# Gated linear attention in a decoder step: the output of a head computed with tokens on the partitions instead of features

## The chip, the cores and the metric

The kernel runs on one core of a Trainium2 chip. It is written by hand in a low-level language: each engine (PE for matrix multiplication, DVE for vectors, ACT for activation functions, POOL for general work, SP for issuing DMAs) has its own list of instructions, which it runs strictly in order, and the lists meet only at semaphores. The metric is the device time of one launch in microseconds (us), from the first to the last instruction with what lies around it. The profile is one execution of the same program, taken by the hardware profiler.

## The reference

The program is one inference step of a two-layer decoder: a layer with gated linear attention (GLA), then a layer with stick-breaking attention over keys and values that eight sampled sequences read from a paged cache. What matters here is the end of the GLA layer, for a prompt of 512 tokens, 4 heads, keys of 128 and values of 256 features per head, in chunks of 64 tokens:

```python
o_intra = jnp.einsum('bhnij,bhnjv->bhniv', att, vc)
chunk_kv = jnp.einsum('bhnck,bhncv->bhnkv', kc * jnp.exp(b_last - b), vc)
def step(s, inp):
    dcy, kv = inp
    return dcy[..., None] * s + kv, s
s_final, s_starts = lax.scan(step, s0, (decay, chunk_kv))     # moveaxis left out
o_inter = jnp.einsum('bhnck,bhnkv->bhncv', q_in, s_starts)
o = o_intra + o_inter
...
o = rms_norm(o, g_out).reshape(B, L, GLA_DV) * jax.nn.silu(g)  # the norm is over the 256 features of a head
return o @ w_out, s
```

So for each head: a causal product inside each chunk, eight states (128 x 256) that follow from one another, their product with the queries, a norm of each token's 256 output features, the gate, and then the product with `w_out`.

## The kernel before

Activations lie feature-major: features on the 128 partitions, the 512 tokens along a row. The program runs in stages of eight products each ("q", "k", "v", "g", "wo0", "ple0", "q1", ...), a product being one tile of 128 output features for all tokens. PSUM has eight banks of 512 float32 columns; the products take banks 0 to 3 in turn, so that up to four of them can wait for DVE to read them, and banks 4 to 7 serve the rest. All matrix products are float32: either split into three fp32r products (line L1562, stages q to g), or done natively in two passes, which the trace shows as two MATMUL records each (L1546 in wo0, ple0, q1; all of the GLA's own products).

The GLA's output is computed inside stage "g". It has eight steps u = 0 to 7 on PE, one product each; head h = u // 2. In an even step PE runs the product, then the output of the head before (`gla_output(h - 1)`) and the scores of head h (`gla_scores`: the decayed keys turned to token-major in bank 4, and `gla_inside` in bank 5). In an odd step it runs the product and then the states of head h (`gla_states`: eight small products of keys with values, four at a time in banks 6 and 7, because the outputs need the same banks), with the square sum of head h - 1 between the two halves (`gla_square_sum`: a product with a matrix of ones, which leaves the sum over the features on every partition of bank 4). The last head's output and square sum lie inside stage "wo0", between pieces of its first products: those need the gated output of a head, feature tile by feature tile (`wait_x`, the semaphore `x_hi`; tiles 0 to 3 are heads 0 and 1, tiles 4 and 5 head 2, tiles 6 and 7 head 3).

DVE in a step: `split_lo` of a weight tile (L1067), `normed` (L1090, the product out of PSUM times the norm), in an odd step `state_steps` (L1272 and L1275: a copy and seven multiply-adds, each waiting for the one before), then `silu` (L1308), then in an odd step `gate_o` of the head before (L1283 to L1287: two products of the output with the norm's factor, two with the gate). In an even step copy_predicated (L1311) masks the scores. Between them DVE scores pages of the key cache for the sampled sequences (`score_pages`, L1244: a reduction of 128 x 1024, and for some pages the multiplication L1243). POOL multiplies most pages with the query (L599) as soon as a page has landed; a page's slot is loaded again once it has been reduced, and four slots serve stage "g". Before the pages of stage wo0 POOL waits for the last head's gate (`gated`), and SP waits for `o_mm` of the last head before it loads pages into the four slots that lie over the GLA's buffers. ACT in an odd step: sigmoid (L689), then `o_rms` of the head before (L823 and L824: Ln, Exp, each with a table load); in an even step sigmoid, `o_copies` of the head before (L816 to L819: two squares, two copies out of banks 6 and 7) and a copy of the turned keys (L850). After step 7: `x_hi` (L662) of tiles 4 and 5, `o_copies` and `o_rms` of the last head, `x_hi` of tiles 6 and 7.

Behind wo0, PE starts ple0 and must add the last square sum (`add_squares(1, KT - 1)`, L1598) before the norm, which DVE and ACT need to go on; in wo0 each product is followed by one such sum.

## Time and profile before

| | us |
|---|---|
| median of 3 runs | 919.36 (919.06 to 919.89) |
| span of the profiled execution, first to last instruction | 917.2 |
| what the median has beyond this span | 2.2 |
| PE busy | 871.6 (95%) |
| DVE busy | 569.6 (62%) |
| ACT busy | 450.9 (49%) |
| POOL busy | 278.1 (30%) |

Times in the rows below are counted from the first instruction of the profiled execution. A row of the timeline merges neighbouring instructions of one line: start, duration, engine, line, operation, what is written from what is read, shape, count, and in square brackets how long the engine stood idle before it and what it waited for. Two neighbouring operations of one engine overlap by some 0.1 us in these rows, so what an operation costs in a sequence is read from start to start. Stage "g" with the GLA's output ends at about 253 us, the first products of wo0 end at 287.7, and ple0's first product ends at about 347.

### The profile page before, as it was taken

How to read it: one execution, taken by the hardware profiler on the slowest of the kernel's cores; microseconds unless marked ns; L12 is line 12 of the kernel's file. 1: busy time of each engine (PE TensorE's matmuls, PEld its weight loads, DVE VectorE, ACT ScalarE, POOL GpSimd, SP SyncE). 2: the span in 40 equal slices, each digit the busy share in tenths (PEclk: the TensorE clock that was granted, in tenths of full speed). 3: DMA queues.
4: the chain of work that ended last, by engine and by line, in shares of the span. 5: the costliest groups of instructions: out<-in, count | busy, mean ns of one | idle time of the engine just before them, and what ended most of it. 6: DMA issues, size and time to landing. Idle time of an engine off the chain costs nothing.

```text
span 917.2 us, 14970 instructions
## 1 busy us (share of the span) xinstructions
PE 871.6 (95%) x5141; PEld 608.2 (66%) x5141; DVE 569.6 (62%) x680; ACT 450.9 (49%) x1521; POOL 278.1 (30%) x148
## 2 busy tenths in 40 slices
PE   5999999989999998999996999999989999999995
PEld 3666777877754444444475887877845554799995
DVE  4555285878957858988998542222167777553553
ACT  4501482324467667568874231221277776434433
POOL 3000002944429997985775000000100000021110
PEclk9989999999999999999998999999999999999997
DMA  9798977752479988888999149989888879321202
GB/s 327 269 374 315 370 235 274 240 179 81 143 235 386 393 292 281 299 294 307 380 330 321 40 147 343 326 315 341 305 317 291 318 267 360 119 92 47 92 1 94
DMA packets 109308, 232.49 MB, mean 253 GB/s; under 512 B 7410, under 2 KB 66425, under 8 KB 109233
## 3 DMA queue, kind: packets, MB, share of 16 engines
q1 hardware_dynamic: 50736, 171.64, 51.6%
q10 hardware_dynamic: 58496, 59.90, 19.6%
q8 instruction: 41, 0.67, 0.3%
q14 instruction: 35, 0.28, 0.1%
HBM read 220.38 MB, written 11.14 MB: 252 GB/s over the span
## 4 chain that ended last, share of the span: by engine, by line
PE 72%; ACT 8%; DVE 7%; DMA 7%; POOL 2%; issue 2%; SPq 1%; ACTq 0%; DVEq 0%; POOLq 0%
PE pp L1559 19%; PE pp L1562 11%; PE pp L1546 10%; PE pp L1970 6%; PE pp L1927 4%; ACT slot L793 3%; PE pp L1543 3%; DMA s<-in_state_gla_dram 3%; DMA slot<-in_cache_k_dram 3%; PE pp L1954 2%; PE pp L1523 2%; POOL slot L599 2%; PE pp L1941 2%; PE pp L1574 1%; PE pp L1639 1%
## 5 line engine op out<-in xcount | busy, mean ns | idle before, releaser
L599 POOL TENSOR_TENSOR slot<-slot,qb 128x1024 f32<-128x1024 f32 x94 | 247.5, 2659 | 128.1 <-DMA slot<-in_cache_k_dram 76.8
L793 ACT ACTIVATE slot<-slot 128x64 f32<-128x64 f32 x480 | 114.8, 241 | 29.5 <-POOL slot L599 29.5
L1244 DVE TENSOR_REDUCE zall<-slot 128x16 f32<-128x1024 f32 x98 | 118.0, 1214 | 11.0 <-POOL slot L599 9.8
L1067 DVE TENSOR_TENSOR w_lo<-w_raw,w_hi 128x1024 fp32r<-128x1024 f32 x57 | 77.5, 1361 | 71.3 <-ACT w_hi L651 71.2
L651 ACT CAST w_hi<-w_raw 128x1024 fp32r<-128x1024 f32 x58 | 60.5, 1044 | 68.1 <-PE pp L1562 26.0
L793 ACT ACTIVATION_READ_ACCUMULATOR slot<-slot 128x1 f32 x480 | 90.0, 188 | 0.0
L1546 PE MATMUL pp<-xn,w_raw 128*128 128x512 f32 x192 | 86.3, 603 | 0.2 <-ACT xn L662 0.2
L1546 PE MATMUL pp<-xn,w_unsplit 128*128 128x512 f32 x192 | 83.9, 592 | 0.0
L1562 PE MATMUL pp<-xa_hi,w_hi 128*128 128x512 f32 x200 | 82.5, 412 | 0.0
L1562 PE MATMUL pp<-xa_hi,w_lo 128*128 128x512 f32 x200 | 80.0, 400 | 0.0
L1562 PE MATMUL pp<-xa_lo,w_hi 128*128 128x512 f32 x200 | 79.7, 399 | 0.0
L1559 PE MATMUL pp<-xb_hi,w_hi 128*128 128x260 f32 x384 | 78.8, 286 | 0.0
L1559 PE MATMUL pp<-xb_lo,w_hi 128*128 128x260 f32 x384 | 77.0, 282 | 0.0
L1559 PE MATMUL pp<-xb_hi,w_lo 128*128 128x260 f32 x368 | 74.0, 283 | 0.0
L1243 DVE TENSOR_TENSOR slot<-slot,qb 128x1024 f32<-128x1024 f32 x34 | 69.9, 2055 | 0.0
L1546 PEld LDWEIGHTS pp<-xn,w_raw 128*128 128x128 f32 x192 | 36.8, 193 | 44.7 <-issue 43.7
L1546 PEld LDWEIGHTS pp<-xn,w_unsplit 128*128 128x128 f32 x192 | 36.5, 190 | 44.2 <-issue 44.0
L1424 DVE TENSOR_TENSOR_SCAN pcum<-pcum,ones 128x256 f32<-128x256 f32 (+1 forms) x64 | 49.3, 813 | 24.8 <-ACT psig L949 24.8
L1970 PE MATMUL pp<-slot,zs 128*32 128x512 f32 x480 | 61.5, 598 | 0.6 <-DVE g1T L1368 0.6
L1559 PEld LDWEIGHTS pp<-xb_hi,w_hi 128*128 128x128 f32 x384 | 59.0, 188 | 1.2 <-issue 0.8
L1559 PEld LDWEIGHTS pp<-xb_lo,w_hi 128*128 128x128 f32 x384 | 59.1, 188 | 0.0
L1090 DVE TENSOR_TENSOR work<-pp,rstd 128x512 f32<-128x512 f32 (+1 forms) x32 | 22.2, 694 | 59.3 <-PE pp L1559 34.4
(302 smaller groups left out, 1516.6 us busy)
## 6 DMA issues: line engine op xcount, KB each, us to landing
slot<-in_cache_k_dram SPq DMA_DIRECT2D x128, 512.0 KB, 6.1
slot<-in_cache_v_dram SPq DMA_DIRECT2D x120, 512.0 KB, 5.3
w_raw<-in_gla_w_in_dram ACTq DMA_DIRECT2D x12, 1024.0 KB, 7.5
slot<-in_gla_w_in_dram SPq DMA_DIRECT2D x24, 512.0 KB, 10.3
w_raw<-in_w_kv_dram ACTq DMA_DIRECT2D x8, 1024.0 KB, 10.5
w_raw<-in_w_ple_gate_dram ACTq DMA_DIRECT2D x6, 1024.0 KB, 5.1
s<-in_state_gla_dram SPq DMA_DIRECT2D x1, 4096.0 KB, 27.2
out_dram<-s ACTq DMA_DIRECT2D x4, 1024.0 KB, 9.3
```

The lines of the kernel that those rows point to most:

```text
L599: nc.gpsimd.tensor_tensor(slot[s][:], slot[s][:], qb[:, (n // NPG) % 2, :], ALU.mult).then_inc(S("k_mul_pool"), 1)
L651: nc.scalar.copy(hi, raw).then_inc(S("w_hi"), 1)
L793: ins = nc.scalar.activation(part, part, ACT.Copy, accum_out=zall[:, n % NPG, b * SH + h:b * SH + h + 1])
L1067: nc.vector.tensor_tensor(lo, raw, hi.bitcast(F32), ALU.subtract).then_inc(S("w_split"), 1)
L1243: own.then(nc.vector.tensor_tensor(at, at, qb[:, b % 2, :], ALU.mult))
L1244: nc.vector.tensor_reduce(zall[:, n % NPG, b * SH:(b + 1) * SH], at.rearrange("p (h d) -> p h d", d=HD), AX.X, ALU.add).then_inc(S("k_used ...
L1424: own.did(nc.vector.tensor_tensor_scan(rev, rev, ones[:, 0:1].to_broadcast([P, n]), 1.0, ALU.mult, ALU.mult))
L1546: last = nc.tensor.matmul(bank[banks_of(j)[0]], w[:, k, :], x[:, 0:NP_TOK], start=(k == 0), stop=(k == KT - 1))
L1559: last = nc.tensor.matmul(pp[m % 2][:, t, 0:H2], w[:, k, :], x[:, t * H2:(t + 1) * H2], start=(k == 0 and first), stop=(k == KT - 1 and w ...
L1562: last = nc.tensor.matmul(bank[banks_of(j)[0]], w[:, k, :], x[:, 0:NP_TOK], start=(k == 0 and first), stop=(k == KT - 1 and w is wl))
L1927: last = nc.tensor.matmul(bank[bk][:, c0:c0 + n], qz[i % 4][:, h % 2, q * P:(q + 1) * P], K1T[:, i, 0:n], start=False, stop=True, skip_gro ...
L1970: last = nc.tensor.matmul(pp[3][32 * g:32 * g + 32, t, :], zs[:, c:c + 32], slot[SLOT_OF[e0 + g]][:, t * 512:(t + 1) * 512], start=(j0 == ...
```

## The change

The output of a head is now made token-major: rows are tokens, columns its 256 features, one block of 128 tokens per half bank (`o_block`). `gla_output` takes the masked scores as the stationary operand and the values as the moving one (4 products of 128 x 256), and then, for each chunk after the first, the queries (64 columns) as stationary and the state (256 columns) as moving operand, written to the 64 partitions of the chunk. ACT's squares, one for each block, also give the sum along the row (`accum_out`), so the product with ones goes; `o_rms` is one Sqrt of 4 numbers per partition. DVE takes the reciprocal and scales the four blocks in place in SBUF (`scale_o`, TENSOR_SCALAR), PE turns them back with eight transposes (`gla_turned`) into banks 4 and 5 (the last head 6 and 7), and `gate_o` is two products that read them from there. Since the square sum and its bank are gone from the odd step, the chunks 4 to 7 of a head get banks 4 and 5, and PE issues the eight state products in one piece.

```diff
         def chunk_bank(c):
-            return bank[6 + c % 2][:, (c // 2 % 2) * HV:(c // 2 % 2 + 1) * HV]
+            return bank[(6 if c < 4 else 4) + c % 2][:, (c // 2 % 2) * HV:(c // 2 % 2 + 1) * HV]
+        def o_block(b):
+            return bank[6 + b // 2][:, (b % 2) * HV:(b % 2 + 1) * HV]
+        def o_rows(h, b):
+            return (qT, kT)[b // 2][:, h, (b % 2) * HV:(b % 2 + 1) * HV]
...
# ACT
                 act.wait_ge(S("o_mm"), h + 1)
-                if h:
-                    act.wait_ge(S("oss_mm"), h)
-                nc.scalar.activation(work[:, 0, 0:NP_TOK], bank[6], ACT.Square)
-                nc.scalar.activation(work[:, 1, 0:NP_TOK], bank[7], ACT.Square).then_inc(S("o_sq"), 1)
+                for b in range(TB):
+                    own.did(nc.scalar.activation(work[:, b // 2, (b % 2) * HV:(b % 2 + 1) * HV], o_block(b), ACT.Square,
+                                                 accum_out=ossq[:, TB * h + b:TB * h + b + 1]))
                 nc.scalar.copy(qT[:, h, :], bank[6])
                 nc.scalar.copy(kT[:, h, :], bank[7]).then_inc(S("o_out"), 1)
             def o_rms(h):
-                act.wait_ge(S("oss_mm"), h + 1)
-                own.then(nc.scalar.activation(gkT[:, h, :], bank[4], ACT.Ln, bias=epsc[:], scale=1.0 / HV))
-                nc.scalar.activation(gkT[:, h, :], gkT[:, h, :], ACT.Exp, scale=-0.5).then_inc(S("o_root"), 1)
+                own.wait()
+                nc.scalar.activation(ort[:, TB * h:TB * h + TB], ossq[:, TB * h:TB * h + TB], ACT.Sqrt, bias=epsc[:],
+                                     scale=1.0 / HV).then_inc(S("o_root"), 1)
...
                     nc.scalar.copy(kdtok[:, h % 2].rearrange("p b n -> p (b n)"), bank[4]).then_inc(S("kd_out"), 1)
-                elif h:
-                    o_rms(h - 1)
+                    if h:
+                        o_rms(h - 1)
+            act.wait_ge(S("st_step"), GH * NCH)
+            o_copies(GH - 1)
+            o_rms(GH - 1)
             act.wait_ge(S("gated"), GH - 1)
             for i in range(4, KT - 2):
                 x_hi(KT + i, gT[:, i, :])
-            act.wait_ge(S("st_step"), GH * NCH)
-            o_copies(GH - 1)
-            o_rms(GH - 1)
             act.wait_ge(S("gated"), GH)
# DVE
+            def scale_o(h):
+                dve.wait_ge(S("o_root"), h + 1)
+                dve.wait_ge(S("o_out"), h + 1)
+                own.then(nc.vector.reciprocal(orstd[:, TB * h:TB * h + TB], ort[:, TB * h:TB * h + TB]))
+                for b in range(TB):
+                    last = nc.vector.tensor_scalar(o_rows(h, b), o_rows(h, b), orstd[:, TB * h + b:TB * h + b + 1], None, ALU.mult)
+                last.then_inc(S("o_n"), 1)
             def gate_o(h):
-                dve.wait_ge(S("o_root"), h + 1)
-                r = gkT[:, h, :]
-                nc.vector.tensor_tensor(qT[:, h, :], qT[:, h, :], r, ALU.mult)
-                own.then(nc.vector.tensor_tensor(kT[:, h, :], kT[:, h, :], r, ALU.mult))
-                for vt, o in enumerate((qT, kT)):
+                dve.wait_ge(S("o_t"), h + 1)
+                for vt in range(2):
                     g = gT[:, 2 * h + vt, :]
-                    last = nc.vector.tensor_tensor(g, g, o[:, h, :], ALU.mult)
+                    last = nc.vector.tensor_tensor(g, bank[(4 if h < GH - 1 else 6) + vt], g, ALU.mult)
                 last.then_inc(S("gated"), 1)
...
                     normed(j, gT[:, u, :])
+                    if h >= 2:
+                        gate_o(h - 2)
                     score_pages(j)
...
                 elif h:
-                    gate_o(h - 1)
+                    scale_o(h - 1)
+            gate_o(GH - 2)
+            scale_o(GH - 1)
             gate_o(GH - 1)
# PE
                 if h >= 2:
-                    pe.wait_ge(S("o_root"), h - 1)
+                    pe.wait_ge(S("gated"), h - 1)
+                if h:
+                    pe.wait_ge(S("st_step"), h * NCH)
...
+            def gla_states(h):
+                pe.wait_ge(S("kd_out"), h + 1)
+                pe.wait_ge(S("att_out"), h + 1)
+                if h:
+                    pe.wait_ge(S("o_out"), h)
+                for c in range(NCH):
...
             def gla_output(h):
                 pe.wait_ge(S("st_step"), (h + 1) * NCH)
+                for b in range(TB):
+                    nc.tensor.matmul(o_block(b), attT[:, h % 2, b * P:(b + 1) * P], vtok[:, b, h * HV:(h + 1) * HV],
+                                     start=(b % 2 == 0), stop=False, skip_group_check=True)
+                for c in range(1, NCH):
+                    r = (c % 2) * CH
+                    last = nc.tensor.matmul(o_block(c // 2)[r:r + CH, :], qT[:, h, c * CH:(c + 1) * CH], states[:, c - 1, :],
+                                            start=False, stop=(c == NCH - 1), skip_group_check=True)
+                last.then_inc(S("o_mm"), 1)
+            def gla_turned(h):
+                pe.wait_ge(S("o_n"), h + 1)
+                if h < GH - 1:
+                    pe.wait_ge(S("st_step"), (h + 2) * NCH)
                 for vt in range(2):
                     for b in range(TB):
+                        last = nc.tensor.transpose(bank[(4 if h < GH - 1 else 6) + vt][:, b * P:(b + 1) * P],
+                                                   o_rows(h, b)[:, vt * P:(vt + 1) * P], ident[:])
+                last.then_inc(S("o_t"), 1)
-            def gla_square_sum(h):
-                pe.wait_ge(S("o_sq"), h + 1)
-                pe.wait_ge(S("kd_out"), min(h + 2, GH))
-                for vt in range(2):
-                    last = nc.tensor.matmul(bank[4], ones[:], work[:, vt, 0:NP_TOK], start=(vt == 0), stop=(vt == 1))
-                last.then_inc(S("oss_mm"), 1)
...
                 if u % 2 == 0:
+                    if h >= 2:
+                        gla_turned(h - 2)
                     if h:
                         gla_output(h - 1)
                     gla_scores(h)
...
-            product(PHASES["wo0"][0], KT, wait_x=True, tiles=range(4))
+            wo = PHASES["wo0"][0]
+            product(wo, KT, wait_x=True, tiles=range(4))
+            gla_turned(GH - 2)
             gla_output(GH - 1)
-            product(PHASES["wo0"][0], KT, wait_x=True, tiles=range(4, 6))
-            gla_square_sum(GH - 1)
-            product(PHASES["wo0"][0] + 1, KT, tiles=range(6))
+            product(wo + 1, KT, tiles=range(4))
             pe.wait_ge(S("p_in"), 16)
+            pe.wait_ge(S("gated"), GH - 1)
             embedded(pin0, 1, 5).then_inc(S("pt"), 1)
-            pe.wait_ge(S("o_root"), GH)
             embedded(pin0, 0, 4).then_inc(S("pt"), 1)
-            product(PHASES["wo0"][0], KT, wait_x=True, tiles=range(6, KT))
-            product(PHASES["wo0"][0] + 1, KT, tiles=range(6, KT))
+            product(wo, KT, wait_x=True, tiles=range(4, 6))
+            product(wo + 1, KT, tiles=range(4, 6))
+            product(wo + 2, KT, tiles=range(6))
+            gla_turned(GH - 1)
+            product(wo, KT, wait_x=True, tiles=range(6, KT))
+            product(wo + 1, KT, tiles=range(6, KT))
+            product(wo + 2, KT, tiles=range(6, KT))
             for u in range(8):
+                if u >= 3:
+                    product(wo + u, KT)
                 if u >= 2:
-                    product(PHASES["wo0"][0] + u, KT)
-                if u:
-                    add_squares(1, u - 1)
+                    add_squares(1, u - 2)
+            add_squares(1, KT - 2)
```

How the lists stand now. On PE, the odd step 5 and the even step 6 of stage "g" (the products L1562, after the change L1580, are left out): before,

```order
L1795 MATMUL pp<-vtok,kdtok 128x256 [waits o_out,kd_out]
L1818 MATMUL pp<-work,ones 128x512 [waits kd_out,o_sq]
L1795 MATMUL pp<-vtok,kdtok 128x256 [waits st_step]
...
L1804 MATMUL pp<-attT,vtok 128x128 [waits st_step,att_out]
L1808 MATMUL pp<-qT,states 128x64 x7
L1804 MATMUL pp<-attT,vtok 128x128 x4
L1808 MATMUL pp<-qT,states 128x64 x7
L1773 MATMUL pp<-ident,kT 128x128 [waits o_root,kdec]
```

and after, where L1813 are the states, L1835 the turning (of the head two back), L1820 and L1824 the output (of the head before), L1793 the turned keys:

```order
L1813 MATMUL pp<-vtok,kdtok 128x256 [waits o_out,att_out,kd_out]
L1813 MATMUL pp<-vtok,kdtok 128x256 x7
...
L1835 MATMUL pp<-ident,qT 128x128 [waits st_step,o_n]
L1835 MATMUL pp<-ident,qT 128x128
L1835 MATMUL pp<-ident,kT 128x128 x2
L1835 MATMUL pp<-ident,qT 128x128 x2
L1835 MATMUL pp<-ident,kT 128x128 x2
L1820 MATMUL pp<-vtok,attT 128x256 [waits st_step]
L1824 MATMUL pp<-states,qT 64x256 x7
L1793 MATMUL pp<-ident,kT 128x128 [waits st_step,gated,kdec]
```

The eight states now stand in one piece, and a wait for DVE's scaling (`o_n`) stands one product behind them.

On DVE, the end of the odd step 3 and the start of step 4: before,

```order
L1275 SCALAR_TENSOR_TENSOR states<-states,dec,pp 128x256 [waits st_step] x3
L1244 TENSOR_REDUCE zall<-slot_82 128x16 [waits k_mul_pool]
L1308 TENSOR_TENSOR gT<-gT,work 128x512 [waits sigm]
L1283 TENSOR_TENSOR qT<-qT,gkT 128x512 [waits o_root]
L1284 TENSOR_TENSOR kT<-kT,gkT 128x512
L1287 TENSOR_TENSOR gT<-gT,qT 128x512 [waits dve_steps]
L1287 TENSOR_TENSOR gT<-gT,kT 128x512
L1067 TENSOR_TENSOR w_lo_54<-w_raw,w_hi_52 128x1024 [waits w_hi]
L1090 TENSOR_TENSOR gT<-pp,rstd 128x512 [waits mm]
```

and after:

```order
L1283 SCALAR_TENSOR_TENSOR states<-states,dec,pp 128x256 [waits st_step] x3
L1252 TENSOR_REDUCE zall<-slot_85 128x16 [waits k_mul_pool]
L1324 TENSOR_TENSOR gT<-gT,work 128x512 [waits sigm]
L1291 RECIPROCAL orstd<-ort 128x4 [waits o_out,o_root]
L1293 TENSOR_SCALAR qT<-qT,orstd 128x256 [waits dve_steps]
L1293 TENSOR_SCALAR qT<-qT,orstd 128x256
L1293 TENSOR_SCALAR kT<-kT,orstd 128x256 x2
L1075 TENSOR_TENSOR w_lo_54<-w_raw,w_hi_52 128x1024 [waits w_hi]
L1098 TENSOR_TENSOR gT<-pp,rstd 128x512 [waits mm]
L1301 TENSOR_TENSOR gT<-pp,gT 128x512 [waits o_t]
```

The scaling, for which PE now waits, stands at the end of the odd step's list, behind the states, the pages and silu; the gate has moved to the next even step of the following head.

## Rows read from the trace of the kernel before

**Rows 1.** The page, part 1: busy time of each engine, share, instructions.

```profile
PE 871.6 (95%) x5141; PEld 608.2 (66%) x5141; DVE 569.6 (62%) x680; ACT 450.9 (49%) x1521; POOL 278.1 (30%) x148
```

**Rows 2.** The timeline of PE, from step 1 of stage g into step 4.

```profile
184.85 1.13 PE L1795 MATMUL pp<-vtok,kdtok 64*128 64x256 f32 x8
188.39 2.03 PE L1795 MATMUL pp<-vtok,kdtok 64*128 64x256 f32 x8 [2.40 <-DVE states L1275]
...
196.74 1.05 PE L1804 MATMUL pp<-attT,vtok 128*128 128x128 f32 x8
...
201.60 0.60 PE L1773 MATMUL pp<-ident,kT 128*128 128x128 f32 x4
...
202.85 0.47 PE L1562 MATMUL pp<-xa_hi,w_hi 128*128 128x512 f32 x1
...
208.62 1.14 PE L1795 MATMUL pp<-vtok,kdtok 64*128 64x256 f32 x8
209.68 1.98 PE L1818 MATMUL pp<-work,ones 128*128 128x512 f32 x4
...
213.02 0.50 PE L1562 MATMUL pp<-xa_hi,w_hi 128*128 128x512 f32 x1
```

**Rows 3.** The windows view: stretch, busy time of each engine, granted clock, DMA.

```profile
188.30:191.50 3.20, 3.11 (x11) 2.10 (x12) 2.13 (x4) 0.00 (x0) 2.09 (x1) 0.53 0.26 69
```

**Rows 4.** The timeline of PE: full and 64-column products, idle times elsewhere.

```profile
280.82 7.03 PE L1546 MATMUL pp<-xn,w_raw 128*128 128x512 f32 x16
...
347.99 1.24 PE L1601 MATMUL pp<-work,ones 128*128 128x260 f32 x4 [2.63 <-ACT work L673]
349.02 8.67 PE L1546 MATMUL pp<-xn,w_raw 128*128 128x512 f32 x16
...
463.24 21.20 PE L1543 MATMUL pp<-xn,w_raw 128*128 128x260 f32 x96
486.14 7.25 PE L1543 MATMUL pp<-xn,w_raw 128*128 128x260 f32 x32 [1.70 <-DVE g1T L1090]
...
686.42 2.38 PE L1954 MATMUL pp<-pat,V 128*64 128x512 f32 x16
```

**Rows 5.** The timeline of DVE in step 3 of stage g.

```profile
211.81 1.21 DVE L1244 TENSOR_REDUCE zall<-slot 128x16 f32<-128x1024 f32 x1
...
216.84 2.88 DVE L1283 TENSOR_TENSOR qT<-qT,gkT 128x512 f32<-128x512 f32 x1
219.65 0.68 DVE L1284 TENSOR_TENSOR kT<-kT,gkT 128x512 f32<-128x512 f32 x1
```

**Rows 6.** The timeline of POOL, step 3 of stage g and stage wo0.

```profile
216.74 2.44 POOL L599 TENSOR_TENSOR slot<-slot,qb 128x1024 f32<-128x1024 f32 x1 [5.88 <-DMA slot<-in_cache_k_dram]
...
275.02 12.60 POOL L599 TENSOR_TENSOR slot<-slot,qb 128x1024 f32<-128x1024 f32 x5 [16.16 <-DVE gT L1287]
...
291.16 54.53 POOL L599 TENSOR_TENSOR slot<-slot,qb 128x1024 f32<-128x1024 f32 x21 [1.00 <-DMA slot<-in_cache_k_dram]
```

**Rows 7.** Groups of DVE and ACT by form: count, busy, mean ns, idle before.

```profile
L1244 DVE TENSOR_REDUCE zall<-slot 128x16 f32<-128x1024 f32 x98 | 118.0, 1214 | 11.0 <-POOL slot L599 9.8
L1473 DVE TENSOR_SCALAR g1T<-hT,gcol 128x520 f32<-128x520 f32 x8 | 3.9, 492 | 0.3
L1485 DVE TENSOR_SCALAR ystage<-ystage,ytok 128x1024 f32<-128x1024 f32 x2 | 1.4, 752 | 0.1
L764 ACT ACTIVATE sgS<-pp 128x256 f32<-128x256 f32 x1 | 0.4, 386 | 4.8 <-PE pp L1713 4.8
```

**Rows 8.** The chain of waits, end of stage g to ple0: start, us, what.

```profile
253.16 1.11 PE pp L1795 x8
...
268.37 1.28 ACT L823
...
335.92 0.87 PE pp L1598 x2
```

**Rows 9.** The timeline of ACT: the square of wo0's last tile.

```profile
329.71 0.61 ACT L673 ACTIVATE work<-hT 128x512 f32<-128x512 f32 x1
```

24 lines of the change are left out of this document (2 added, 22 removed).

## The prediction

> **What bounds the kernel now.** The first view to read is the page's busy time: PE is busy for 871.6 of 917.2 us [rows 1], so in most stages a microsecond of PE work, or of PE idling, is a microsecond of the result. The timeline of PE in stage g confirms it for the place of the change: from 184.85 to 213.02 the operations follow one another, and the one idle time that stands out, 2.40 us, lies before the second half of a head's states [rows 2]. The chain of waits from the end of stage g to ple0 then stays on PE but for one turn through ACT and DVE for the last head's norm and gate [rows 8], and it takes 335.92 - 253.16 = 82.8 us from the last states to the square sum in ple0. So the change is costed on PE's list: work removed, work added, and the new waits. DVE has room in total, but its list is strictly in order, and one of the new waits hangs on the end of a piece of it. I call "odd step" the stretch that begins with a head's states and "even step" the one that begins with an output.
>
> **What it removes on PE.** The square sum and the split of the states: an odd step has 213.02 - 208.62 = 4.4 us between two products [rows 2]; eight states in one piece are twice 209.68 - 208.62 = 1.06, so 2.1. Gain 2.3 us. In step 1 more goes: from 184.85 to the output at 196.74 are 11.9 us [rows 2], because the idle 2.40 us also cost the clock (0.53 granted in the stretch behind it, its lower level, after 1.00 before [rows 3]). After the change these are states 2.1 and a product 5.8 (208.62 - 202.85), so 7.9. Gain 4.0 us. DVE does not take it back: its last state of that head ends before PE's product does, since the second half of the states no longer waits for PE.
>
> The output itself: 201.60 - 196.74 = 4.9 us before [rows 2]. Now it is 8 records of 256 columns on the whole array, at 21.20 / 96 = 0.22 us each for 260 columns [rows 4], 1.7 us, and 14 records with 64 stationary columns. Such records run in pairs: 16 of them with 320 columns on average took 2.3 us [rows 4], against 16 x 0.27 on the whole array, so about 0.53 of the price; 14 x 0.22 x 0.53 = 1.6. Sum 3.4, gain 1.5 us per head, four times. The bounds are the full price (14 x 0.22 = 3.1, a gain of nothing) and a perfect pairing (1.8 in all less). I take the middle value, which is of the same kind of instruction.
>
> The Trainium skill, "TensorEngine Tiling (Array Packing)", Key Properties, says that changing the tiling mode drains the engine, and the change adds two such changes per head. The 64-column records at 686.42 end inside 2.38 us with their modes changed on both sides [rows 4], so nothing more than a tenth of a microsecond can hide there, and the sum would not move.
>
> **What it adds on PE.** Eight transposes per head: four take 0.60 with their overlap at 201.60 [rows 2], so 0.9 us for eight.
>
> **The wait for the scaling in steps 4 and 6.** This is the term that decides. PE comes to the turning 2.1 + 5.8 = 7.9 us after its states began. DVE's list in the odd step is normed, eight states, two pages, silu, and then the scaling. In step 3 before the change, silu was over and the next operation began at 216.84, which is 8.2 us after the states began at 208.62 [rows 5, 2]; splitting the states or not leaves this as it is, because DVE spends the time of PE's square sum on the page between the two halves. Behind it stand the reciprocal with its semaphore (some 0.3) and four TENSOR_SCALAR of 256 columns: from 492 ns at 520 and 752 ns at 1024 columns [rows 7], 0.36 each or 0.27 start to start, 1.2 in all. Undisturbed, the last scaled block is there at 9.7, and PE idles 1.8 us.
>
> But POOL starts to multiply the next page at 216.74, 0.1 us before the scaling could start [rows 6], and that is no accident of one step: the page's load is released by the reduction in the middle of the same list, which ends at 211.81 + 1.21 = 213.0, 3.7 us earlier [rows 5], so POOL and the scaling come up together again after the change. The DVE operation that stood there, a product of two SBUF tensors, took 2.88 us where its neighbour of the same size took 0.68 [rows 5]: it sat out POOL's multiplication. The 98 reductions, which read one tensor from SBUF, average 1214 ns [rows 7], though POOL was active beside many of them, so none is held. What TENSOR_SCALAR does beside POOL this trace does not show. Its bounds are no delay (as the reduction) and 2.2 us (as L1283). I take 2.2, because it is nearer to that row in what it draws from SBUF: 0.52 ns a column, less than half of the reduction's 1.18, so two elements at a time, as the product of two tensors does. Then the scaled blocks are there at 8.2 + 2.2 + 1.2 = 11.6, PE idles 3.7 us.
>
> The Trainium skill, "SBUF — State Buffer", Who interferes with whom, states what the trace lacks: a DVE instruction in a two-port mode, which tensor_scalar from SBUF to SBUF can enter, takes a port pair that GpSimd also uses, and whoever comes first holds it for the whole instruction. By that rule the 2.2 us stand; the part of the rule on two SBUF inputs and on tensor_reduce agrees with the rows above.
>
> An idle time of this length costs clock as well: after 2.63 us of idling, 16 records took 8.67 instead of 7.03 us [rows 4], 1.6 more; after 1.70 us, 32 records took 7.25, the usual 0.22 each [rows 4], nothing. So each of these two waits costs 3.7 + 1.6.
> Per odd and even step together: -2.3 - 1.5 + 0.9 + 3.7 + 1.6 = +2.4 us, twice (steps 3 and 4, steps 5 and 6), +4.9 us. The other new waits of these steps are covered: `gated` before the turned keys (DVE has the 3.4 us of the output for two operations of 0.7), `att_out` and `o_out` before the states (a product of 5.8 lies before them; ACT's longer `o_copies` fits with some 1 us to spare).
>
> **The tail, from the last states on (0 = 253.16 before).** States 2.1; four tiles of the first wo0 product 3.5 (7.03 for 16 records); at 5.6 PE waits for the scaling of head 2. POOL is done with its pages of stage g here, so 9.7. Idle 4.1, clock 1.6; turning 0.9, output 3.4: 15.6. Four tiles of the second product 3.5, embedding 0.9: 20.0. ACT meanwhile needs from 15.6: four squares with sums (386 ns for 256 columns [rows 7], 1.6 with the sums read out), two copies 1.0, table load 1.3 [rows 8], square root 0.3, and `x_hi` 0.7, since the change puts `o_copies` ahead of it: 20.5. Two tiles of two products 3.5, six tiles of the third 5.2, turning 0.9: 30.1. Now nothing is left to cover the gate: two operations 1.4, `x_hi` 0.8, idle 2.2 us. That lies between the 1.70 that cost no clock and the 2.40 that did; I put 1.0 for it. Six tiles 5.2: 38.5. Five products, the embedding's products, six tiles of ple0 and seven square sums of 0.9 follow without a gap, 48.9 (before: from the end of the third product at 280.82 + 7.03 - 0.16 = 287.7 [rows 4] to 335.9 [rows 8] 48.1 with the rows unrounded, and one square sum more stands behind it now): 87.4, against 82.8. So +4.6 us, between +4.0 and +5.2.
> A second bound on this stretch: POOL starts the pages of wo0 with the gate of the last head (275.02) and then works without a pause up to 345.7 [rows 6]; ACT's last square, which follows these pages, is ready 55.3 us after that start [rows 9]. The gate is now at 31.5, so 86.8: just covered. What lay 5 us apart before now ties.
>
> **The sum.** Step 1 and its output -4.0 - 1.5 = -5.5; steps 3 to 6 +4.9; the rest +4.6 (its output's gain is inside). Total +4.0 us. Downstream nothing takes it up: ple0 and what follows start from that square sum, and the page work of ACT and DVE behind it is reached in order, after it. 917.2 + 4.0 and the 2.2 us that the median has beyond the span: 923.5 us.
>
> **The rivals.** *No block by POOL* (0.22): the scaling is not held, or comes ahead of POOL by a tenth. Then each pair of steps is -2.3 - 1.5 + 0.9 + 1.8 = -1.1, the total -5.5 - 2.2 + 4.6 = -3.0, 916.4 us: faster. For it: the race is decided by 0.1 us, and no row shows a held TENSOR_SCALAR. Against: its rate. *One of the two steps only* (0.12): +0.5, 919.9 us, no change. *The change doesn't do what it says* (0.04): the 64-column records of two chunks do not run in pairs, since they write different banks in turn; +1.5 four times, 929.3 us. Against it stands L1954. *Something worse* (0.06): the fourth scaling also falls behind the following page, 2.2 us more in each step, up to 928.
> The change ends on the fast side if DVE's scaled blocks come before about 9.8 us in steps 3 and 5; it ends on the slow side if they come behind POOL's page.
>
> **How the numbers follow.** Forecast with the block in both steps 0.56, at 923.5, by itself 921.5 to 926 (clock after the 2.2 us idle, pairing). 0.2% of the time, 1.8 us, is about what a measurement of this kernel can tell from no change: faster is under 917.5, slower over 921.2. Slower: 0.50 of the forecast, 0.03 of the single block, 0.07 of the rest: 0.60. Faster: 0.18 of the unblocked case and 0.03 elsewhere: 0.21. Same: 0.19. The range 915.5 to 927.5 takes in the unblocked case and leaves out about 0.1 on either side.
>
> **What the profile after would show.** L1813 in one piece of 2.1 us, no idle before it; L1820 and L1824 together 3.4 us; PE idle before L1835 3.7 us in steps 4 and 6, about 4 in wo0, with a granted clock near 0.5 behind it; one L1293 of each of steps 3 and 5 at 2 us instead of 0.36, beside a POOL operation that started before it; 2.2 us idle of PE before the seventh tile in wo0. If L1293 shows 0.36 everywhere the central step is wrong and the time should be near 916; if PE idles before L1835 for less than 1 us, my reading of DVE's list is wrong.

## The result and the profile after

| | before | after |
|---|---|---|
| median, us (runs) | 919.21 (917.06 to 919.89, 4) | 928.78 (926.53 to 932.72, 4) |
| ratio, 95% interval | | 1.0111 (1.0084 to 1.0139) |
| span of the profiled execution | 917.2 | 929.1 |
| forecast | | 923.5, range 915.5 to 927.5 |

The change costs 10 us. The direction was right, the size was not: the median lies outside the range. The medians differ by 9.6 us and the two profiled executions by 11.9, because the profiled execution of the kernel after is one of 930.8 us, 2 us above its median. The first table to make is where these 11.9 us arise, stretch by stretch, from start to start of the same operations on PE.

| stretch on PE | before | after | difference | forecast |
|---|---|---|---|---|
| first states to the states of step 3 (the first states start 0.5 sooner) | 184.85, 208.62 | 184.38, 202.77 | -5.9 in all | -5.5 |
| to the states of step 5 | 230.97 | 229.97 | +4.9 | +2.4 |
| to the states of step 7 | 253.09 | 254.39 | +2.3 | +2.4 |
| to the square sum in ple0 (wo0) | 335.75 | 343.25 | +6.2 | +4.6 |
| to ple0's second square sum (ple0's turn) | 359.25 | 367.79 | +1.0 | 0 |
| to the sum of the last page (q1, g1) | 499.68 | 510.85 | +2.6 | 0 |
| to the end | 917.2 | 929.1 | +0.7 | 0 |

The timeline of PE after, the answer to [rows 2] and [rows 4]. L1813 are the states, L1820 and L1824 the output, L1835 the turning:

```profile
184.38 2.00 PE L1813 MATMUL pp<-vtok,kdtok 64*128 64x256 f32 x16 [0.21 <-DVE attT L1327]
...
192.01 1.89 PE L1820 MATMUL pp<-vtok,attT 128*128 128x256 f32 x8
193.83 1.94 PE L1824 MATMUL pp<-states,qT 128*64 128x256 f32 x14
...
216.45 0.69 PE L1835 MATMUL pp<-ident,qT 128*128 128x128 f32 x2 [5.89 <-DVE kT L1293]
...
241.38 0.69 PE L1835 MATMUL pp<-ident,qT 128*128 128x128 f32 x2 [3.61 <-DVE kT L1293]
```

The states in one piece take 2.0 us, step 1 has no idle time any more, and the output takes 3.7 us (192.01 to 195.70, where the turned keys start) instead of 4.9. All of that is as forecast. The two waits before the turning are there too, but one of them is 5.9 us and not 3.7. The timeline of DVE shows why; it answers [rows 5]:

```profile
210.96 2.76 DVE L1293 TENSOR_SCALAR qT<-qT,orstd 128x256 f32<-128x256 f32 x2
213.65 2.75 DVE L1293 TENSOR_SCALAR kT<-kT,orstd 128x256 f32<-128x256 f32 x2
...
238.17 2.62 DVE L1293 TENSOR_SCALAR qT<-qT,orstd 128x256 f32<-128x256 f32 x2
240.72 0.61 DVE L1293 TENSOR_SCALAR kT<-kT,orstd 128x256 f32<-128x256 f32 x2
...
262.77 0.62 DVE L1293 TENSOR_SCALAR qT<-qT,orstd 128x256 f32<-128x256 f32 x2
```

Two scalings take 0.62 us undisturbed (262.77), and 2.6 to 2.8 us in three of the four pairs of steps 3 and 5. POOL, in step 3 and at the start of wo0's pages, the answer to [rows 6]:

```profile
210.98 2.34 POOL L608 TENSOR_TENSOR slot<-slot,qb 128x1024 f32<-128x1024 f32 x1 [3.42 <-DMA slot<-in_cache_k_dram]
213.91 2.34 POOL L608 TENSOR_TENSOR slot<-slot,qb 128x1024 f32<-128x1024 f32 x1 [0.59 <-DMA slot<-in_cache_k_dram]
...
286.37 14.91 POOL L608 TENSOR_TENSOR slot<-slot,qb 128x1024 f32<-128x1024 f32 x6 [31.83 <-DVE gT L1301]
```

In step 3 a second page follows 0.6 us behind the first and holds the second pair too. The windows view (stretch, busy time of PE, PEld, DVE, ACT, POOL, granted clock, DMA share, GB/s) shows the clock behind the first wait, as [rows 3] did: 0.59 on average, so mostly the lower of its two levels, and then 1.00:

```profile
216.40:221.10 4.70, 4.65 (x18) 3.90 (x20) 4.38 (x6) 1.58 (x2) 0.00 (x0) 0.59 0.35 91
...
221.10:229.90 8.80, 8.80 (x51) 6.68 (x50) 3.35 (x4) 4.60 (x13) 4.31 (x2) 1.00 0.55 206
```

The last third of the loss lies where the forecast had nothing. The view of PE's waits (what was waited for: us in total, times, longest), of before and then of after:

```profile
PE pp L1895 <- DVE zall L1244: 6.3, 1, 6.3
...
PE pp L1543 <- DVE g1T L1090: 1.7, 1, 1.7
```

```profile
PE pp L1835 <- DVE kT L1293: 13.4, 3, 5.9
...
PE pp L1619 <- ACT work L682: 3.7, 1, 3.7
PE pp L1561 <- DVE g1T L1098: 3.3, 1, 3.3
PE pp L1918 <- DVE zall L1252: 2.9, 1, 2.9
```

Before, PE waited 8.0 us in g1 for DVE. So in the kernel before PE was already ahead there, and something else set when the last page of the key cache was summed. That "something" is what the forecast left out, and most of the experiments are about it.

### The profile page after: what moved, and what is told of

Its sections match the earlier page's. It is cut to its first block, busy times and chain, and to the rows that moved or that the text cites. A ratio compares the mean times of both kernels' runs of the same rounds, so it can differ in the third digit from the quotient of the medians.

```text
span 929.1 us, 14856 instructions
## 1 busy us (share of the span) xinstructions
PE 868.2 (93%) x5069; PEld 603.6 (65%) x5069; DVE 572.2 (62%) x692; ACT 445.2 (48%) x1538; POOL 280.9 (30%) x148
## 4 chain that ended last, share of the span: by engine, by line
PE 72%; DVE 11%; ACT 6%; DMA 6%; issue 3%; SPq 1%; POOL 0%; ACTq 0%; DVEq 0%; POOLq 0%
PE pp L1577 18%; PE pp L1580 12%; PE pp L1564 11%; PE pp L1993 6%; PE pp L1950 4%; PE pp L1561 3%; DVE slot L1251 3%; DMA s<-in_state_gla_dram 3%; PE pp L1541 2%; ACT slot L802 2%; PE pp L1977 2%; DVE zall L1252 2%; PE pp L1964 2%; PE pp L1592 1%; DMA slot<-in_cache_v_dram 1%
## 5 line engine op out<-in xcount | busy, mean ns | idle before, releaser
L608 POOL TENSOR_TENSOR slot<-slot,qb 128x1024 f32<-128x1024 f32 x94 | 250.2, 2687 | 135.0 <-DMA slot<-in_cache_k_dram 68.0
L1252 DVE TENSOR_REDUCE zall<-slot 128x16 f32<-128x1024 f32 x98 | 117.9, 1214 | 10.7 <-POOL slot L608 9.4
L1580 PE MATMUL pp<-xa_hi,w_hi 128*128 128x512 f32 x200 | 82.0, 410 | 0.0
L1580 PE MATMUL pp<-xa_hi,w_lo 128*128 128x512 f32 x200 | 79.2, 396 | 0.0
L1580 PE MATMUL pp<-xa_lo,w_hi 128*128 128x512 f32 x200 | 79.0, 395 | 0.0
L1251 DVE TENSOR_TENSOR slot<-slot,qb 128x1024 f32<-128x1024 f32 x34 | 76.5, 2249 | 0.0
L1442 DVE TENSOR_TENSOR_SCAN pcum<-pcum,ones 128x256 f32<-128x256 f32 (+1 forms) x64 | 49.3, 812 | 24.8 <-ACT psig L957 24.8
## 6 DMA issues: line engine op xcount, KB each, us to landing
w_raw<-in_w_kv_dram ACTq DMA_DIRECT2D x8, 1024.0 KB, 10.7
```

What stands on the lines that cost most here:

```text
L608: nc.gpsimd.tensor_tensor(slot[s][:], slot[s][:], qb[:, (n // NPG) % 2, :], ALU.mult).then_inc(S("k_mul_pool"), 1)
L1251: own.then(nc.vector.tensor_tensor(at, at, qb[:, b % 2, :], ALU.mult))
L1252: nc.vector.tensor_reduce(zall[:, n % NPG, b * SH:(b + 1) * SH], at.rearrange("p (h d) -> p h d", d=HD), AX.X, ALU.add).then_inc(S("k_used ...
L1442: own.did(nc.vector.tensor_tensor_scan(rev, rev, ones[:, 0:1].to_broadcast([P, n]), 1.0, ALU.mult, ALU.mult))
L1580: last = nc.tensor.matmul(bank[banks_of(j)[0]], w[:, k, :], x[:, 0:NP_TOK], start=(k == 0 and first), stop=(k == KT - 1 and w is wl))
```

## The experiments

All of them are compared with the kernel before (medians 917.9 to 918.9 in the four sets; single runs of it lie between 913.4 and 923.1). For each the text on record comes first.

### The same kernel in more runs

> The kernel after, unchanged, in more runs beside those of the kernel before, because the runs of one kernel spread over 6 us and the first comparison had four of each. If the first figure holds: 926 to 932 us, 9 to 11 more than before. If it was a chance of few runs: a median below 926.

Measured: 929.48 us (926.22 to 931.04, 6 runs), ratio 1.0108 (1.0084 to 1.0133). The loss is 10 to 12 us. In the profile the scaling of step 3 is held twice again and PE waits 5.9 us.

### Is it POOL that holds the scaling?

```diff
-                        nc.gpsimd.tensor_tensor(slot[s][:], slot[s][:], qb[:, (n // NPG) % 2, :],
+                        w = 1 if PHASES["g"][0] <= job < PHASES["wo0"][0] else D
+                        nc.gpsimd.tensor_tensor(slot[s][:, 0:w], slot[s][:, 0:w], qb[:, (n // NPG) % 2, 0:w],
```

> The kernel after, with POOL multiplying one column instead of 1024 of each page whose turn falls in stage g. The rest of these pages stays unmultiplied, so work is left out; loads, waits and orders are the same. It asks whether the long TENSOR_SCALAR (2.76 us for two of 256 columns in step 3, twice, and 2.62 in step 5) come from POOL's multiplication beside them. Theory A (held by POOL): every pair of L1293 takes 0.62 us, the idle times of PE before the turning in steps 4 and 6 fall from 5.9 and 3.6 us to about 1.3, without a loss of clock, so states to states takes about 20.8 us instead of 27.2 and 24.4. The tail stays. About 10 us less than the kernel after: 919 us. Rival B (the long ones are a cost of the form, or of the data coming from ACT): the L1293 stay at 2.6 to 2.8 us and the time stays within 0.3% of 928.8.

Measured: 921.96 us (12 runs), 6.8 less than the first median of the kernel after and 7.5 less than the second; 10 were expected. DVE in steps 3 and 5, and the wait of PE behind the second:

```profile
211.82 0.62 DVE L1294 TENSOR_SCALAR qT<-qT,orstd 128x256 f32<-128x256 f32 x2
212.35 0.61 DVE L1294 TENSOR_SCALAR kT<-kT,orstd 128x256 f32<-128x256 f32 x2
...
232.91 0.62 DVE L1294 TENSOR_SCALAR qT<-qT,orstd 128x256 f32<-128x256 f32 x2
```

```profile
234.11 0.44 PE L1836 MATMUL pp<-ident,qT 128*128 128x128 f32 x2 [1.61 <-DVE kT L1294]
```

No scaling is held when POOL has next to nothing to do beside it: it is POOL, rival B is out. The wait that is left, 1.6 us, is the place in the list alone (the forecast had 1.8), and it costs no clock: the stretch from 213.0 to 217.6 has a granted clock of 1.00. States to states takes 21.1 us in both pairs of steps, as theory A had it (20.8). The Trainium skill, "SBUF — State Buffer", Who interferes with whom, says of tensor_scalar, copy and cast that they can enter a two-port mode, and that whoever issues first then has the pair for the whole instruction; these rows agree, with 0.62 us alone and up to 2.8 us behind a POOL operation of 2.34.

### The scaling at the start of the odd step's list

```diff
                 if u % 2:
                     split_lo(j + 1)
+                    if h:
+                        scale_o(h - 1)
                     normed(j, gT[:, u, :])
...
-                elif h:
-                    scale_o(h - 1)
```

> The kernel after, with DVE's scaling of a head moved from the end of the odd step's list to its start, between the split of the weight tile and the norm of the product, where the trace of the kernel after shows DVE idle for 2.2 to 4.8 us (before the three L1098 of steps 3, 5, 7) and the root already there (ACT's Sqrt ended at 200.53, the product's norm began at 202.87). Theory A (the loss is PE's wait for a scaling that stands at the end of DVE's list): the three waits before the turning, 5.9, 3.6 and 3.9 us, go, and with them the low clock behind them. The stretch from states to states falls from 27.2 and 24.4 to about 19.5 us (7.7 and 5.0 less), the tail loses 5.4, in all 18 us: about 911 us. Rival B (the wait only changes its name: with 1.4 us more ahead of the norm, DVE's states come later, and PE waits for the last state before the turning or the output): 1 to 2 us of idle time in each of the three places, with L1283 as the releaser, and 917 to 922 us. Rival C (what costs is the new form of the output on PE, not the waits): within 0.3% of the kernel after, about 928.

Measured: 917.3 us (910.1 to 919.9, 12 runs), ratio to before 0.9971 (0.9947 to 0.9995). Rival B had the time right, and the releaser (DVE's states) in two of its three places; theory A did not hold:

```profile
220.59 2.75 DVE L1293 TENSOR_SCALAR qT<-qT,orstd 128x256 f32<-128x256 f32 x2
223.26 2.71 DVE L1293 TENSOR_SCALAR kT<-kT,orstd 128x256 f32<-128x256 f32 x2
...
241.25 4.83 DVE L1293 TENSOR_SCALAR qT<-qT,orstd 128x256 f32<-128x256 f32 x2
```

```profile
231.67 0.41 PE L1835 MATMUL pp<-ident,qT 128*128 128x128 f32 x2 [1.21 <-DVE states L1283]
...
251.37 0.66 PE L1835 MATMUL pp<-ident,qT 128*128 128x128 f32 x2 [2.33 <-DVE states L1283]
```

In steps 5 and 7 the scaling is held again, at its new place, and now it delays the states behind it. The new place is better (states to states 19.3 and 20.7 us instead of 27.2 and 24.4), because less hangs on it. But look at where the gain goes. The square sum in ple0 starts at 331.44, 4.3 us sooner than before. The sum of the last page starts at 499.59, and before at 499.68. PE's lead is gone by then; it waits for the pages in g1 (4.0 us for the last sum alone).

### The turning of the last head one product sooner

```diff
+            gla_turned(GH - 1)
             product(wo + 2, KT, tiles=range(6))
-            gla_turned(GH - 1)
```

> The kernel after, with the turning of the last head moved ahead of the six tiles of the third wo0 product instead of behind them. The trace of the kernel after shows its scaling done at 275.9 and PE at this place at about 278.8, so nothing is waited for, and 5.2 us of products then cover the gate. Theory A (the later gate costs twice, on PE in wo0 and through POOL's later pages in ple0 and q1): the idle 2.2 us before the seventh tile and the 1.7 us of low clock behind it go, POOL starts its pages of wo0 5 us sooner (26.8 instead of 32.0 us after the last states), so the add of ple0's turn is held no longer (1.75 us back to about 0.7) and q1 and g1 take some 1 to 2.6 us less than their 72.0: 5 to 7 us in all, 922 to 924. Rival B (what ple0, q1 and g1 lost has nothing to do with POOL's start): only the 3.9 us on PE in wo0 come back, 925, and the stretches behind the square sum in ple0 keep their 25.3 and 72.0 us.

Measured: 926.3 us (923.7 to 926.9, 6 runs), 2.5 to 3.2 less than the two medians of the kernel after, a smaller gain than either theory gave. In the profile the idle time before the seventh tile and the clock behind it are gone (the square sum in ple0 at 338.76, 4.5 us sooner), and the sum of the last page comes at 504.83, 6.0 sooner than after. Theory A's claim on ple0's turn fell: PE still waits 3.67 us there. Behind that sum 2.0 of the 6.0 us are lost again, 1.4 of them in the product that follows it (9.11 instead of 7.75 us for 32 records), which now stands behind an idle time of 5.7 us in one piece.

### POOL's pages later, nothing else

```diff
                     pool.wait_ge(S("gated"), GH)
+                    pool.wait_ge(S("mm"), tiles_through(j + 2))
```

> The kernel before, where POOL's pages of wo0 wait not only for the last gate (275.0) but also for the end of the third wo0 product (287.7), 12.7 us later; nothing on PE or in the GLA is changed. In the kernel after they began 11.3 us later than before. Theory A (POOL's start sets a second bound, 55.3 us to the square of wo0's last tile, and its backlog then costs in ple0 and q1): that square is ready at 343.0, so the square sum of ple0 moves from 335.9 to about 343.5, the add of ple0's turn is held by POOL (0.7 becomes 1.5 or more), and q1 and g1 take 1 to 3 us more than their 69.4: 9 to 12 us more, 928 to 931. Rival B (POOL has slack, as its 30% of busy time say; PE's list is the only bound in wo0): within 2 us of the kernel before, 919 to 921.

Measured: 930.24 us (927.8 to 934.5, 6 runs), ratio 1.0132 (1.010 to 1.0163): as slow as the kernel after, with not one instruction of the GLA changed.

```profile
295.52 2.07 PE L1599 MATMUL pp<-work,ones 128*128 128x512 f32 x2 [7.64 <-ACT work L674]
```

```profile
510.60 1.97 PE L1896 MATMUL pp<-ident,zall 128*128 128x128 f32 x8 [6.28 <-DVE zall L1245]
```

Rival B is out: 30% of busy time is no slack. The stream of pages starts 13 us late and ends 10.9 us late. It reaches PE at another place than theory A had it: DVE waits 11.3 us in one piece for a page of POOL's, and PE 7.6 us behind it in wo0, at 295.52, so the square sum in ple0 comes at 346.47, 10.7 us later than before (7.6 were expected).

### POOL's pages sooner

```diff
-                if j == PHASES["wo0"][0]:
-                    pool.wait_ge(S("gated"), GH)
```

> The kernel after, where POOL's pages of wo0 no longer wait for the last head's gate. The pages that have landed by then (the first six, 14.9 us of POOL) are multiplied up to 20 us sooner. DVE's own part of these pages stands behind its first residual add in wo0 (289.71), which does not move. Theory A (DVE's residual and POOL's start bound the stream of pages together; with POOL ahead, DVE keeps PE's pace of 7.72 us a step in wo0 instead of 7.93 and is not 6 us behind at its end): the sum of the last page comes 5 to 6 us sooner than at 510.9, ple0's turn holds no add, 922 to 925. Theory A' (POOL's start alone is the clock of the stream, 224 us to its end): the sum of the last page comes 10 us or more sooner, PE becomes the bound, 918 to 920. Rival B (POOL's pages now fall on the scaling and the gate of heads 2 and 3 and hold them as in step 3): PE waits 2 to 5 us more before the turning in wo0, 928 or more.

> The kernel before, where POOL's pages of wo0 do not wait for the last head's gate. Here DVE's first residual add ends at 278.5, 3.5 us after POOL's start, and DVE's add for wo0's last tile comes 1.2 us behind PE's product (after: 6 us). Theory A (both bound the stream): POOL gets ahead, but DVE can gain only these 1 to 2 us: 916.5 to 919. Theory A' (POOL's start alone is the clock): the sum of the last page comes 6 us or more sooner and the 8 us that PE waits in g1 shrink by as much: 911 to 913. Rival B (POOL holds the norm products and gates of heads 2 and 3, L1283 to L1287): up to 3 us more, 920 to 922.

Measured: the kernel after without this wait 930.73 us (6 runs), the kernel before without it 922.6 us (11 runs; ratio 1.006, 1.0035 to 1.0085). After: POOL starts 12 us sooner (274.40), and the sum of the last page comes at 510.02 instead of 510.85. So POOL's start alone is not the clock either; A' is out, and A's 5 us did not come. Rival B had the time (928 or more), but not its reason: no wait before the turning is longer than in the kernel after (3.7, 3.7 and 3.9 us). Before: POOL now falls on the last head's gate, as rival B had it (its 920 to 922 were slightly too low),

```profile
276.15 2.72 DVE L1285 TENSOR_TENSOR gT<-gT,qT 128x512 f32<-128x512 f32 x1
278.79 2.82 DVE L1285 TENSOR_TENSOR gT<-gT,kT 128x512 f32<-128x512 f32 x1
```

(0.69 each in the kernel before), and PE waits 4.4 us for the tiles that it gives. The wait on the gate is there for a reason.

What paces the pages shows when the kernels are laid side by side. These are starts in the profiled executions: DVE's first residual add in wo0 (which follows the end of the first wo0 product, and behind which DVE's first pages of wo0 stand), POOL's first page of wo0, and the sum of the last page.

```
kernel                residual   POOL    last page   from residual  from POOL
before                  277.8    275.0    499.7         221.8         224.7
after                   289.7    286.4    510.9         221.1         224.5
after, again            290.5    287.2    511.0         220.5         223.8
e2_small_pool           280.6    277.8    501.0         220.4         223.3
e1_early                277.7    273.7    499.6         221.9         225.9
e3_turn_sooner          286.5    281.0    504.8         218.3         223.8
e4_before_pool_late     277.9    288.0    510.6         232.7         222.6
e8_after_nogate         287.3    274.4    510.0         222.8         235.6
e9_before_nogate        286.3    275.7    507.2         220.9         231.5
e5_psum (below)         271.6    267.1    487.8         216.2         220.7
e6_psum_turn (below)    268.2    262.7    485.9         217.7         223.2
e13_two_pieces (below)  282.2    276.7    500.7         218.5         224.0
```

The last page is summed 216 to 223 us after the residual add, whatever PE does between, unless POOL starts behind that add (e4_before_pool_late); a POOL that starts 13 us ahead of it brings nothing (e8_after_nogate). POOL's start is as good a mark where POOL waits for the last gate: 220.7 to 225.9 us in these ten profiles. So the stream needs both, and between the kernel before and the kernel after the two moved together (11.9 and 11.3 us), so which of them is the later one there is not told apart.

### What paces the stream

In the kernel before, with one column instead of 1024 in DVE's own 34 multiplications, and, in a second kernel, in POOL's from wo0 on (the rest of the pages stays unmultiplied):

```diff
-                        own.then(nc.vector.tensor_tensor(at, at, qb[:, b % 2, :], ALU.mult))
+                        own.then(nc.vector.tensor_tensor(at[:, 0:1], at[:, 0:1], qb[:, b % 2, 0:1], ALU.mult))
```

```diff
-                        nc.gpsimd.tensor_tensor(slot[s][:], slot[s][:], qb[:, (n // NPG) % 2, :],
+                        w = 1 if job >= PHASES["wo0"][0] else D
+                        nc.gpsimd.tensor_tensor(slot[s][:, 0:w], slot[s][:, 0:w], qb[:, (n // NPG) % 2, 0:w],
```

> The kernel before, with DVE multiplying one column instead of 1024 in the 34 pages that are its own (69.9 us of busy time in the trace of before); the rest of these pages stays unmultiplied, so work is left out. It asks what paces the stream of pages from DVE's first residual add in wo0 (277.84) to the sum of the last page (499.68), 221.8 us, in which DVE is busy for 194.5 and POOL for 183.7 us and the DMA queues at 0.92. Theory A (DVE's list paces it): the sum of the last page is no longer late, and the 1.7 and 6.3 us that PE waits in g1 go, with about 1 us of clock: 909 to 911 us, PE's own list then being the bound. Rival B (the loads pace it): the sum comes as late as before, PE waits in g1 as long, 917 to 920. Rival C (POOL paces it): the same as B, with POOL without idle time in q1 and g1.

> The kernel before, with POOL multiplying one column instead of 1024 of its pages from wo0 on (work is left out), so that nothing holds DVE's products of two SBUF tensors there. Theory A (DVE's list paces the stream, and POOL acts on it by holding it): DVE's 34 multiplications take 1.2 us each instead of a mean of 2.06, some 29 us less in all, and nothing waits for POOL; the waits in g1 go as in e11_dve_light, 909 to 911. Rival B (the loads pace it): the waits in g1 stay within 2 us of 8.0, 916 to 920. If only one of these two kernels is faster, it names the engine.

Measured: 909.08 us (6 runs) and 906.24 us (5 runs), ratios 0.9895 (0.9871 to 0.9919) and 0.9862 (0.9836 to 0.9889). PE at the sum of the last page, in the first and in the second:

```profile
491.68 1.09 PE L1895 MATMUL pp<-ident,zall 128*128 128x128 f32 x8 [0.51 <-DVE zall L1244]
```

```profile
492.34 1.04 PE L1896 MATMUL pp<-ident,zall 128*128 128x128 f32 x8
```

Of the 8.0 us of waiting in g1 0.5 are left in the first and nothing in the second. The sum of the last page comes 212.4 and 211.8 us after the residual add instead of 221.8, and no load took the place of the waits, so the loads are not what held it at 221.8 (whether they would at 212 was not tested). But both kernels are faster, so by the recorded text the pair names neither engine alone. Nor did the first leave POOL's time as it was. POOL's 94 multiplications took 247.5 us in the kernel before (2659 ns each), and in the first kernel

```profile
L599 POOL TENSOR_TENSOR slot<-slot,qb 128x1024 f32<-128x1024 f32 x94 | 226.1, 2431 | 142.6 <-DMA slot<-in_cache_k_dram 90.0 <-DMA qb<-q_rows 35.3 <-DVE gT L1287 17.2
```

so DVE's multiplications hold POOL's as POOL's hold DVE's. What paces the pages is the work of the two together. Two stretches of the kernel before, one in wo0 and one in q1 (columns as in the windows view above), show which of them is full where:

```profile
300.00:320.00 20.00, 20.00 (x48) 8.86 (x47) 16.90 (x14) 12.80 (x91) 20.00 (x8) 1.00 1.04 392
440.00:460.00 20.00, 20.00 (x48) 8.93 (x47) 19.45 (x12) 17.43 (x146) 15.61 (x6) 1.00 1.00 374
```

In wo0 POOL is busy all the time (20.00 of 20 us, DVE 16.90), and DVE waits for it; in q1 DVE's list is nearly full (19.45) and POOL is not (15.61). The second kernel shows what POOL does to DVE's list:

```profile
L1244 DVE TENSOR_TENSOR slot<-slot,qb 128x1024 f32<-128x1024 f32 x34 | 41.3, 1216 | 0.8 <-DMA slot<-in_cache_k_dram 0.8
```

where the same 34 operations took 69.9 us in the kernel before. How much of the gain of the second kernel is this and how much is that DVE never waits for a page that POOL has yet to multiply, these two runs don't separate.

### The scaling out of POOL's way

The gate reads PSUM, and in e1_early it took its usual 1.28 us beside a POOL operation. So the scaling reads PSUM too:

```diff
-                nc.scalar.copy(qT[:, h, :], bank[6])
-                nc.scalar.copy(kT[:, h, :], bank[7]).then_inc(S("o_out"), 1)
...
-                dve.wait_ge(S("o_out"), h + 1)
...
-                    last = nc.vector.tensor_scalar(o_rows(h, b), o_rows(h, b), ...
+                    last = nc.vector.tensor_scalar(o_rows(h, b), o_block(b), ...
...
-                    pe.wait_ge(S("o_out"), h)
+                    pe.wait_ge(S("o_n"), h)
```

> The kernel with the scaling at the start of the odd step's list (e1_early), where DVE now reads the unscaled blocks from PSUM and writes the scaled ones to SBUF; ACT's two copies of them go, and the next states wait for the scaling instead of the copies. In e1_early the scaling of steps 5 and 7 was held by POOL's pages (2.75, 2.71 and 4.83 us for two blocks instead of 0.62), the states came late, and PE idled 1.2 and 2.3 us before the turning. The gate's product of PSUM and SBUF (L1301) took its usual 1.28 us at 234.90 beside a POOL operation from 233.29 to 238.96, so an operand in PSUM seems to exempt from being held. Theory A: no L1293 over 0.8 us for two blocks, no idle before the turning, states every 19.3 us; POOL's pages of wo0 start near 268 us instead of 273.7. And since in the kernels run so far the sum of the last page ends 223 to 226 us after this start, whatever PE does (before 224.7, after 224.5, e1_early 225.9, e3 223.8, e4 222.6), it ends near 492 us instead of 499.6, and the time falls by about 7 us, to 910. Rival B (held as well: reading PSUM changes nothing): 916 to 918. Rival C (PE's list and not the stream of pages sets the end): PE gains 1.2 + 2.3 us and 1.4 of clock, 912, and the waits of PE in g1 stay as in e1_early.

> e5_psum and the turning of the last head ahead of the third wo0 product's six tiles (as in e3_turn_sooner), so that the gate and with it POOL's start come 5 us sooner and the 2.2 us of idle and 1.7 us of low clock before the seventh tile go. Theory A (POOL's start plus 224 us is the sum of the last page): start near 263, sum near 487, 905 us. Rival C (PE's list): 3.9 us less than e5_psum. Rival D (by now neither: the pages' loads or DVE's own list): no more than 1 us less than e5_psum.

Measured: 911.28 us (6 runs), ratio 0.9927 (0.9898 to 0.9956), and 907.38 us (906.5 to 910.3, 5 runs), ratio 0.9888 (0.9856 to 0.992). DVE and POOL of the first in step 5:

```profile
219.21 0.88 DVE L1290 TENSOR_SCALAR qT<-pp,orstd 128x256 f32<-128x256 f32 x2
220.00 0.87 DVE L1290 TENSOR_SCALAR kT<-pp,orstd 128x256 f32<-128x256 f32 x2
```

```profile
220.26 4.72 POOL L608 TENSOR_TENSOR slot<-slot,qb 128x1024 f32<-128x1024 f32 x2 [3.50 <-DMA slot<-in_cache_k_dram]
```

Undisturbed it is dearer (0.88 us for two instead of 0.62), and no pair took longer in either kernel, though those of steps 5 and 7 ran beside POOL's pages. The Trainium skill, "VectorE: DVE Perf Modes", Why PSUM operands drop a tier, states a reason: the two-port mode needs both SBUF read ports, and PSUM has one read port for DVE. These rows agree, with 0.88 us for two against 0.62 and no hold. PE has no idle time before the turning, states follow each other in 19.3 us, and the residual add comes at 271.6 and 268.2; the last page is summed at 487.8 and 485.9 (expected 492 and 487). Both times are within 1.3 and 2.4 us of what was expected from the start of the stream. They do not decide against rival C. From PE's list alone e5_psum would have been 912, too close to tell apart by the time, and PE's waits in g1 are 7.8 us in e5_psum and 7.4 in e1_early, so they stayed, as rival C had it. The profiles say little more: the sum of the last page comes 11.8 us sooner than in e1_early, but the profiled execution is the slowest of e1_early and the fastest of e5_psum, and the medians differ by 6.0. What is shown is that the scaling is no longer held and that the kernel is faster than e1_early (911 against 917 us); ACT's two copies went with the same edit, and what they were worth is not separated.

### One part of the change undone

The last kernel with the states in two pieces again:

```diff
-            return bank[(6 if c < 4 else 4) + c % 2][:, (c // 2 % 2) * HV:(c // 2 % 2 + 1) * HV]
+            return bank[6 + c % 2][:, (c // 2 % 2) * HV:(c // 2 % 2 + 1) * HV]
...
                 for c in range(NCH):
+                    if c == 4:
+                        pe.wait_ge(S("st_step"), h * NCH + 4)
```

> e6_psum_turn with one part of the change undone: the chunks 4 to 7 of a head go back to the banks of chunks 0 to 3, so PE issues four states, waits for DVE to have read them, and issues four more. Nothing lies between the halves now. In e6_psum_turn DVE's fourth state ends at 206.9 and PE's first half would end at about 204.8, so PE idles 2.1 to 2.4 us in each of the four odd steps. Theory A (as the kernel before showed at 188.39, an idle time of this length also costs 1.6 us or more of low clock): 4 us in each step, 16 us in all, and since all of it lies ahead of DVE's first residual add in wo0, from which the sum of the last page comes 218 us later, all of it reaches the end: about 923 us. Rival B (idle time only, no clock): 9 to 10 us, 917. Rival C (the product behind the second half was not on the path, the pages in g1 set the end): under 5 us, 909 to 912.

Measured: 921.78 us (919.6 to 925.9, 12 runs), 14.4 more than e6_psum_turn, ratio to before 1.0031 (1.0011 to 1.0051).

```profile
210.58 1.14 PE L1812 MATMUL pp<-vtok,kdtok 64*128 64x256 f32 x8 [2.20 <-DVE states L1281]
...
233.86 1.14 PE L1812 MATMUL pp<-vtok,kdtok 64*128 64x256 f32 x8 [2.20 <-DVE states L1281]
...
255.60 1.32 PE L1812 MATMUL pp<-vtok,kdtok 64*128 64x256 f32 x8 [2.20 <-DVE states L1281]
256.85 5.16 PE L1561 MATMUL pp<-xn,w_raw 128*128 128x512 f32 x8
```

Theory A holds in the sum: the residual add comes 14.0 us later (282.2), and all of it reaches the end. In the parts it is rougher: four idle times of 2.2 to 2.4 us, and the same 2.20 us cost 1.5 us of clock in wo0 (5.16 instead of 3.67 us for eight records) and in step 3, but nothing in step 5; nor did 2.36 us in step 1 (0.2 at most). So the two halves of the change belong together. The square sum that the token-major output saves had covered the wait between the two pieces of states; without it the pieces cost more than the output saves, and only the eight states at once make the rest a gain.

## Why the forecast was right and where it failed

**Work on PE.** Right. Eight states 2.0 us (2.1 forecast), step 1 7.6 us to its output (7.9), the output 3.7 us (3.4), eight transposes 0.9. That two chunks of 64 columns run in pairs is confirmed: the 14 records took 1.87 us, where full price is 3.1.

**The wait before the turning.** The mechanism was right and is shown by e2_small_pool: TENSOR_SCALAR in SBUF is held by POOL, and PE waits for it. With one block the wait was 3.6 us in step 6 of the kernel after, 3.8 and 3.6 in e3_turn_sooner, 3.7 twice in e8_after_nogate: the forecast's 3.7. The mis-sized term is step 4 of the kernel after, 5.9 instead of 3.7 us: I priced one block by POOL, and the second was the rival with 0.06. Yet the four scalings need 0.8 us from the first start to the last, and the second page came 0.6 us behind the first in the kernel after (POOL at 213.91 behind 210.98 + 2.34). In the trace of before that gap had been 1.0 us, so the margin was 0.2, and I had not worked it out. With the page decided by the DMA queue, the second block was far likelier than 0.06; it came in two of the four profiles that share this code (after, and again), not in the other two (e3_turn_sooner, e8_after_nogate). That is +2.2 us of the 7.9 by which the span (+11.9) exceeds the forecast (+4.0).

**The clock.** 1.6 us for an idle time of 3.7 was fair: 1.4 to 1.9 us in the kernel after, though 2.6 in step 4 of e3_turn_sooner. For the 2.2 us before the seventh tile I put 1.0, and it was 1.8 (12 records in 6.9 us instead of 5.15). e13_two_pieces shows that one length of idle time has no one price.

**The tail on PE.** 88.9 us measured, 87.4 forecast: 0.8 of that is the clock just named and 0.4 an idle time of 0.43 us at 275.27, where PE waits for a tile of head 2. The second bound, POOL's, was priced at 55.3 us behind the gate and as covered, and PE does not wait for ACT's square there (the pauses of POOL that it left out are 0.2 and 1.0 us in the timeline of before).

**"Downstream nothing takes it up."** This is the step that failed. The total of +4.0 is the delay of the square sum in ple0; that delay was 7.5, for the reasons above (3.5 us), and the other 4.4 us of the 7.9 arose behind it, where the forecast put nothing. It let all that follows start from that sum. Up to DVE's first norm in ple0 this is so: the norm waits for the root of the sum in both kernels, and comes 7.5 us later after the change. Before and after:

```profile
339.48 0.69 DVE L1090 TENSOR_TENSOR work<-pp,rstd 128x512 f32<-128x512 f32 x1 [3.98 <-ACT rstd L686]
```

```profile
346.97 0.69 DVE L1098 TENSOR_TENSOR work<-pp,rstd 128x512 f32<-128x512 f32 x1 [0.21 <-ACT rstd L695]
```

But the page work is not simply "reached in order, after it". The pages were later than that, by 11.9 us at DVE's residual add and 11.3 at POOL's first page, and from the norm to the sum of the last page DVE now needs 163.9 us instead of 160.2: its 27 multiplications there take 60.7 instead of 53.6 us, and it waits 3.3 us less for others. So behind ple0's norm it was the work on the pages, and not PE's list, that set the sum of the last page; e1_early shows the same from the other side, with its square sum 4.3 us sooner than before and its last page at the same time. The 8.0 us that PE waited for DVE in g1 stood in the timeline that I had read ([rows 4] has the 1.70, the 6.3 came two rows on), and I used them for the clock alone.

Taken along this path, the forecast's own walk comes closer. The last two tiles of the first product end 34.5 us after the last states (30.1, 2.2 of idle, 1.7 for two tiles, 0.5 of clock), and before, DVE's add stood 277.84 - 253.09 = 24.8 us behind them. With the -0.6 us by which the last states were to move, that is +9.1, and 928.5 us; by POOL's start (the gate at 31.5 instead of 21.9) it is +9.0. That this meets the median is in part luck: the add moved by 11.9 us, since the walk lacks the second block, and the profiled execution lies 2 us above the median.

The agreement has its limits. The time from the residual add to the last page lies between 216 and 223 us in eleven profiles, so a forecast made this way is good to some 3 us; and why it is 216 in e5_psum and 223 in e8_after_nogate stays open. How much of it is DVE's list and how much POOL's is not shown either, since each run that made one lighter made the other shorter too. Single runs of one kernel spread over 4 to 10 us, and the race between POOL and DVE for each page, which falls out differently with each kernel, may be part of it; that was not tested.

## What to carry to other kernels

An engine that is busy for 95% is not for that reason the path. Where it waits for other engines late in the program, its own work ahead of that wait has slack, up to the length of the wait, as far as those engines do not wait for it. The delay to cost is then that of their work: look in several profiles for the operation from which the time to that wait is constant, and forecast that operation's start. And a new wait for a DVE operation should be put on one that POOL can't hold; an operand in PSUM does that here, for 0.13 us an operation.

## What the runs showed of the hardware

A TENSOR_SCALAR of 128x256 float32 in SBUF takes 0.27 us from start to start, and was held by a POOL product beside it until that ended, so that two took 2.6 to 2.8 and once 4.8 us; with its input in PSUM it takes 0.40 us and was not held in e5_psum or e6_psum_turn. A DVE product of one column took 0.75 us in the mean of 34 in e11_dve_light: 16 of them 0.20 us or less, others up to 2.18 (at 292.74, beside a POOL product that started at 292.55), so making the held operation smaller does not free it. POOL's products are held by DVE's in turn: a mean of 2659 ns in the kernel before, 2431 in e11_dve_light. The same idle time of PE, 2.20 us, was followed by a low clock twice and once not (e13_two_pieces).
